# A decoder layer on one core: router logits summed inside the output projection, and expert ranks found on 32 partitions

## The chip, the cores and the metric

The kernel runs on one core of one Trainium2 chip and is written by hand, engine by engine, with semaphores between the engines. The metric is the time of one execution in device microseconds (us). TensorE (PE) multiplies matrices and also transposes 128x128 tiles by a product with an identity; PEld is its weight load. VectorE (DVE), ScalarE (ACT) and GpSimd (POOL) do elementwise work, and SyncE (SP) issues most transfers. Matrix products write to PSUM, eight banks of 128 partitions by 512 float32. Everything else lives in one SBUF array called `arena`; all data are float32.

## The reference

One layer on 512 tokens of width 2048. `h = x + mix(rms_norm(x)) @ w_out`, where `mix` concatenates three token mixers (attention, a state-space layer, a gated recurrence). Then a mixture of experts reads `hn = rms_norm(h, ffn_norm_g)`:

```
gl = hn @ w_group            # 4 groups;  g_idx = argmax
el = hn @ w_router           # 32 experts, 8 in a group
top 2 experts inside the best group; gates = softmax of the two, times p_g
h += sum over the two experts of gate * (silu(hn @ w_gate[e]) * (hn @ w_up[e])) @ w_down[e]
out = rms_norm(h, final_norm_g)
```

The experts' weights are 32 x 3 x 4 MB. All of them are read from HBM once.

## The kernel before, in words

The work is one long sequence of steps (`steps`), walked by every engine in the same order; each engine does its part of a step. PE's products of the input and output projections are laid out in *gaps*: seven products make one pair of column chunks (a Strassen-like scheme, `("pr", p, n)`, line 843 for the output projection), and other steps are hung behind chosen products.

- **Output projection.** Eight pairs `WO_P`, chunks of 128 columns of `h`, each added by DVE to `H0` (rows of tokens, four tiles of 128 tokens by 2048). After a pair, ACT squares its 128 x 128 pieces and accumulates their sums (line 1288). DVE also forms the weight sums of the next products (line 521).
- **Norm and router.** Behind the last pair come DVE's sum of the squares (L1866), ACT's square root (L1367), and for each of four token tiles DVE's `h * rstd * g` into a row buffer `HSB` (L1874). SP writes each row buffer to HBM as `hs_rows` (L611), PE turns it in 16 transposes (L1042, step `hT`), ACT copies these to `HNT` (L1203). Step `rt` (L1048) multiplies the 16 chunks by the router's 36 columns, DVE copies the result (L1883), step `rT` (L1053) turns it back to tokens on partitions, DVE copies it to `RLG` (L1886).
- **Routing on DVE.** Group argmax, two expert argmaxes, one-hots (`onehots_ready`); gates; counts per expert from a product (`rk`, L1059); the *rank* of each expert by count, found on all 128 partitions as a 32 x 32 comparison and a row sum (three instructions, L1931 to L1933); a second 32 x 32 comparison that turns ranks into the order in which experts are loaded (L1422, L1940, L1941, `order_ready`); places of tokens (`id`, L1065) and `slots_ready` (L1997).
- **Experts.** SP waits for `order_ready` and then streams the weights through eight slots of 2 MB (L590); a slot is loaded again when PE has used it. A big and a small expert share a tile of 128 slots: 16 tiles, gate and up (L1124), down (L1143). POOL gathers each tile's rows of `hs_rows` (L763) after `slots_ready`; PE turns them (L1099), DVE copies them from PSUM (L2004), and PE returns results to tokens (`combine`, L1086).

The row buffers, the turned chunks and the router's columns lie where the experts' slots come later.

Of the kernel before, what the change touches and what calls it, by code (L numbers as in the profile page):

```python
# [82 lines left out]
def build(nc, d, out, cc):  # L83

    ctx = ExitStack()
    with ctx:
# [28 lines left out]
        def take(n):  # L115
            at[0] += n
            return at[0] - n
# [7 lines left out]
        LBL, D5, SUB, HNG = take(HH), take(NB5), take(1), take(1)  # L125
# [15 lines left out]
        NPK = KD + 2 * HH + 2  # L141
        assert HNG + 1 - GMIX == NPK
# [70 lines left out]
        JUNK, SSP = AQ + 4 * HB, AQ + 4 * HB + P  # L213
# [4 lines left out]
        HNT = SLOT[6]  # L218
        GF, HSB = E0 + 2048, [E0, E0 + 4096]
        assert SSP + TB * 16 <= GF  # L220
        RLT = GF
        WR = W - KD * 36
# [9 lines left out]
        RKY, RRK, RNB, RSQ, RCP, RBS, RORD = (take(NE) for _ in range(7))  # L232
        RKS, RPX = take(TB * NE), take((TB + 1) * NE)
        assert at[0] <= WR
# [141 lines left out]
        for s in steps:  # L376
# [12 lines left out]
            for x in new:  # L389
# [7 lines left out]
                  "hT", "rt", "rT", "rk", "id")  # L397
# [3 lines left out]
        for at_, s in enumerate(steps):  # L401
            if s[0] == "pq":
                small = [0, 1, 2, 3]
            elif s[0] == "al":
                small, ticking = [0, 1, 2], True
            elif s[0] == "hT":
                small = [0, 1, 2, 3, 4, 5, 6, 7]
# [45 lines left out]
        x_again, h_std, gf_in, hs_ready = sem("x_again"), sem("h_std"), sem("gf_in"), sem("hs_ready")  # L453
        hs_out = [sem("hs_out0"), sem("hs_out1")]
# [108 lines left out]
        def _(sp):  # L563
# [28 lines left out]
            for i in range(len(blocks)):  # L592
# [10 lines left out]
                elif blocks[i][0] == ("wo", 4, 0):  # L603
                    see_copy(sp, ("az", AH - 1))
                    see_copy(sp, ("pr", WO_P[0], 6))
                    sp.dma_start(F(WR, KD * 36), DV(d["router"], 0, [(KD * 36, P), (1, KD * 36)])).then_inc(router_in, 16)
                    sp.dma_start(F(GF, D), DV(d["ffn_norm_g"], 0, [(0, P), (1, D)])).then_inc(gf_in, 16)
                load(i)
            for t in range(TB):
                sp.wait_ge(hs_ready, t + 1)  # L610
                sp.dma_start(DV(hs_d, t * P * D, [(D, P), (1, D)]), F(HSB[t % 2], D)).then_inc(hs_out[t % 2], 16)  # L611

            see_bank(sp, ("rt",))
# [25 lines left out]
        def _(pool):  # L639
# [109 lines left out]
            for s in hs_out:  # L749
                pool.wait_ge(s, 32)  # L750
# [41 lines left out]
        def _(pe):  # L792
# [58 lines left out]
            def do(s):  # L851
# [43 lines left out]
                if kind == "pj":  # L895
# [7 lines left out]
                    return  # L903
                if s not in use:
                    return
# [132 lines left out]
                elif kind == "hT":  # L1038
                    t, q = s[1:]
                    once(hs_ready, t + 1)  # L1040
                    for c in range(4):
                        last = tr(B(bank, [(1, P)], off=c * P), V(HSB[t % 2] + 4 * q + c, [(KD, P)]), ident)  # L1042
                elif kind == "rt":
                    once(router_in, 16)
                    for q in range(16):
                        once_copied(("hT", q // 4, q % 4))
                    for k in range(KD):
                        last = mm(B(bank, [(1, S)], 0, 36), F(WR + k * 36, 36), F(HNT + k * S, S),  # L1048
                                  start=(k == 0), stop=(k == KD - 1))
# [147 lines left out]
        def _(act):  # L1197
# [40 lines left out]
            def do(s):  # L1238
# [29 lines left out]
                elif kind == "fin":  # L1268
# [4 lines left out]
                    for k, j in PAIRS[p]:  # L1273
# [10 lines left out]
                        elif k == "wo":  # L1284
                            for t in range(TB):
                                if j or t:
                                    act.wait_ge(squares_done, j * TB + t)
                                A(F(JUNK, P), F(H0 + t * D + j * P, P), ACT.Square,
                                  accum_out=F(SSP + t * 16 + j, 1)).then_inc(squares_done, 1)
# [66 lines left out]
                elif kind == "hT":  # L1356
                    t, q = s[1:]
                    evac(s, V(HNT + 4 * q * S + t * P, [(S, 4), (1, P)]), ([(P, 4), (1, P)],))

# [4 lines left out]
            for s in steps:  # L1364
                if s == ("hT", 0, 0):
                    act.wait_ge(squares_sum, 1)
                    A(F(STD, TB), F(SSQ, TB), ACT.Sqrt, scale=1.0 / D, bias=F(EPSC, 1)).then_inc(h_std, 1)  # L1367
# [39 lines left out]
        def _(dve):  # L1407
# [367 lines left out]
            def do(s):  # L1775
# [86 lines left out]
                elif kind == "hT" and s[2] == 0:  # L1862
                    t = s[1]
                    if t == 0:
                        dve.wait_ge(squares_done, 16 * TB)
                        v.tensor_reduce(F(SSQ, TB), V(SSP, [(16, TB), (1, 16)]), AX.X, AD).then_inc(squares_sum, 1)  # L1866
                        dve.wait_ge(gf_in, 16)
                        dve.wait_ge(h_std, 1)
                        settle(v.reciprocal(F(RST, TB), F(STD, TB)))
                    if t >= 2:  # L1870
                        dve.wait_ge(hs_out[t % 2], 16)
# [236 lines left out]
```

## Time and profile before

| | us |
|---|---|
| median of 3 runs (2052.52 to 2056.9) | 2055.41 |
| the profiled execution | 2060.28 |
| its span, first to last instruction | 2058.4 |
| end of the last output-projection product | 961.3 |
| first load of expert weights | 1019.6 |
| first expert product | 1049.16 |
| last combine begins | 2028.5 |

Busy shares over the span: PE 93%, DVE 40%, ACT 13%, POOL 9%. HBM moves 251 GB/s on average, but above 410 GB/s from 1020 us to about 2000 us. A time such as 1019.6 is counted from the first instruction of the span.

### The profile page before, as it was taken

The page shows a single profiled execution, that of the slowest core. Times are in us where ns is not written, and L with a number is a line of the kernel's source. Part 1 is how long each engine was busy: PE and PEld are TensorE (multiplying, and loading weights), DVE is VectorE, ACT ScalarE, POOL GpSimd, SP SyncE. Part 2 cuts the span into 40 slices and gives each one's busy share as a digit, 9 for nine tenths or more (in the row PEclk, how much of TensorE's full clock was granted, in tenths as well). Part 3 has the DMA queues.
Part 4 walks back from the last instruction along what each step waited for, and adds up shares of the span by engine and source line. Part 5 has one row for each costly group of instructions (what it writes and reads, how often), then busy time and mean ns, then how long its engine had stood idle before and what let it go on. Part 6 is the DMA issues. An engine that isn't in the chain of part 4 may idle for free.

```text
span 2058.4 us, 32623 instructions
## 1 busy us (share of the span) xinstructions
PE 1906.0 (93%) x13671; PEld 1183.1 (57%) x13671; DVE 821.7 (40%) x1531; ACT 259.6 (13%) x626; POOL 189.1 (9%) x218
## 2 busy tenths in 40 slices
PE   6999999999998979998468999999999999999996
PEld 4888999699987869998122333333333323333332
DVE  6666685176465543333511222212222312222215
ACT  3012112100334231112000000000000000000002
POOL 1353332000000000000010000000000000000000
PEclk9999999999999999999689999999999999999998
DMA  5243333211121233222299999999999999999992
GB/s 208 88 141 99 83 94 96 91 52 60 64 72 47 67 128 109 82 83 78 92 423 425 425 422 423 420 419 422 414 421 406 423 422 411 424 411 423 420 387 105
DMA packets 74419, 508.53 MB, mean 247 GB/s; under 512 B 19200, under 2 KB 19348, under 8 KB 38176
## 3 DMA queue, kind: packets, MB, share of 16 engines
q1 hardware_dynamic: 56720, 486.34, 58.4%
q0 software_dynamic: 5728, 15.81, 2.3%
q10 hardware_dynamic: 11824, 4.17, 1.1%
q8 instruction: 123, 2.02, 0.4%
q14 instruction: 24, 0.20, 0.0%
HBM read 504.26 MB, written 12.99 MB: 251 GB/s over the span
## 4 chain that ended last, share of the span: by engine, by line
PE 77%; DMA 13%; DVE 5%; issue 3%; ACT 2%; SPq 0%; POOL 0%; DVEq 0%; ACTq 0%; POOLq 0%
PE psum L1124 19%; PE psum L843 19%; PE psum L846 15%; DMA arena<-in_moe_w_gate 11%; PE psum L1086 9%; PE psum L1143 6%; PE psum L988 2%; DVE arena L1422 2%; DMA arena<-in_moe_w_down 1%; PE psum L900 1%; PE psum L1099 1%; PE psum L1048 1%; DMA arena<-hs_rows,arena 1%; DVE arena L1425 1%; PE psum L977 0%
## 5 line engine op out<-in xcount | busy, mean ns | idle before, releaser
L1124 PE MATMUL psum<-arena 128*32 128x512 f32 x4096 | 465.9, 608 | 32.6 <-issue 15.9
L843 PE MATMUL psum<-arena 128*128 128x128 f32 x3584 | 411.0, 277 | 2.6 <-issue 2.6
L843 PEld LDWEIGHTS psum<-arena 128*128 128x128 f32 x3584 | 407.8, 194 | 4.1 <-issue 3.6
L1422 DVE TENSOR_TENSOR arena<-psum,arena 128x512 f32<-128x512 f32 x290 | 198.9, 689 | 417.1 <-PE psum L1086 413.9
L1124 PEld LDWEIGHTS psum<-arena 128*32 128x32 f32 x4096 | 135.1, 112 | 355.4 <-issue 354.2
L846 PE MATMUL psum<-arena 128*128 128x256 f32 x1456 | 324.7, 382 | 1.9 <-DVE arena L521 1.4
L846 PEld LDWEIGHTS psum<-arena 128*128 128x128 f32 x1456 | 275.1, 191 | 40.7 <-issue 3.9
L1422 DVE TENSOR_TENSOR arena<-arena,psum 128x256 f32<-128x256 f32 (+2 forms) x174 | 76.5, 439 | 434.9 <-PE psum L843 206.9
L1086 PE MATMUL psum<-arena 128*128 128x512 f32 x512 | 236.0, 605 | 0.9 <-issue 0.9
L1143 PE MATMUL psum<-arena 128*32 128x512 f32 x2048 | 225.9, 599 | 5.7 <-DMA arena<-in_moe_w_down 5.3
L1422 DVE TENSOR_TENSOR arena<-arena 128x128 f32<-128x128 f32 (+17 forms) x448 | 180.1, 443 | 39.8 <-ACT arena L1203 31.3
L1086 PEld LDWEIGHTS psum<-arena 128*128 128x128 f32 x512 | 92.3, 190 | 145.3 <-issue 145.3
L1143 PEld LDWEIGHTS psum<-arena 128*32 128x32 f32 x2048 | 66.6, 111 | 152.9 <-issue 149.7
L521 DVE TENSOR_TENSOR arena<-arena 128x1024 f32<-128x1024 f32 x116 | 148.7, 1282 | 2.5 <-DVE arena L1422 1.3
L775 POOL TENSOR_SCALAR arena<-arena 128x512 f32<-128x512 f32 x16 | 33.3, 2080 | 864.9 <-PE psum L1086 864.6
L2024 DVE COPY arena<-psum 128x512 f32<-128x512 f32 x16 | 11.1, 691 | 190.3 <-PE psum L1143 190.3
L1384 ACT ACTIVATE arena<-psum 128x512 f32<-128x512 f32 x16 | 9.6, 598 | 387.4 <-PE psum L1108 387.4
L1267 ACT ACTIVATE arena<-psum 128x256 f32<-128x256 f32 x50 | 18.9, 378 | 284.9 <-PE psum L846 202.2
L1203 ACT ACTIVATE arena<-psum 128x512 f32<-128x512 f32 (+3 forms) x81 | 38.6, 507 | 110.1 <-PE psum L977 28.8
L1099 PE MATMUL psum<-arena 128*128 128x128 f32 x272 | 37.7, 284 | 14.7 <-DMA arena<-hs_rows,arena 14.7
L1099 PEld LDWEIGHTS psum<-arena 128*128 128x128 f32 x272 | 35.6, 195 | 22.9 <-issue 22.9
L2004 DVE COPY arena<-psum 128x512 f32<-128x512 f32 x68 | 42.4, 681 | 15.1 <-PE psum L1099 15.1
(187 smaller groups left out, 989.1 us busy)
## 6 DMA issues: line engine op xcount, KB each, us to landing
arena<-in_moe_w_gate SPq DMA_DIRECT2D x64, 2048.0 KB, 26.7
arena<-in_moe_w_up SPq DMA_DIRECT2D x64, 2048.0 KB, 26.4
arena<-in_moe_w_down SPq DMA_DIRECT2D x64, 2048.0 KB, 26.3
arena<-in_w_in SPq DMA_DIRECT2D x86, 512.0 KB, 4.6
arena<-in_w_out SPq DMA_DIRECT2D x32, 512.0 KB, 4.7
arena<-in_x SPq DMA_DIRECT2D x8, 1024.0 KB, 8.2
hs_rows<-arena SPq DMA_DIRECT2D x4, 1024.0 KB, 4.0
out<-arena SPq DMA_DIRECT2D x4, 1024.0 KB, 4.0
```

Of the source, the lines that this page charges most:

```text
L521: e.tensor_tensor(F(o, BLK), F(a, BLK), F(b, BLK), ALU.subtract).then_inc(sums_ready, 1)
L775: g.tensor_scalar(F(SEL, S), F(IOTA, S), F(SELP, 1), F(SELP + 1, 1), ALU.is_equal, ALU.mult).then_inc(sel_ready, 1)
L843: last = mm(B(bank, [(1, P)], off=t * P), F(a + t * P, P), F(w + i * P, P), start=start and t == 0, stop=(i == KH - 1), skip_group_check=True)
L846: last = mm(B(bank, [(1, HB)]), F(w + i * P, P), F(a, HB), start=start, stop=(i == KH - 1), skip_group_check=True)
L988: last = mm(B(bank, [(1, P)], off=t * P), F(KT + h * S + t * P, P), F(QT + h * S + t * P, P), start=True, stop=True)
L1086: mm(B(4 + q, [(1, 512)]), F(SEL + t * P, P), F(YSB + q * 512, 512), start=True, stop=True).then_inc(comb_full, 1)
L1099: last = tr(B(TURN_BANK[f], [(1, CAP)], off=c * CAP), V(XG[par] + 4 * f + c, [(KD, P)], 0, CAP), ident)
L1124: last = mm(B(bank, [(1, FE)], 32 * g, 32), F(XT + c * CAP + 32 * g, 32), F(SLOT[slot] + (c % 8) * FE, FE), start=(c == 0), stop=(c == KD ...
L1143: last = mm(B(4 + q, [(1, 512)], 32 * g, 32), F(HTE + m * CAP + 32 * g, 32), F(SLOT[slot] + (m % 2) * D + q * 512, 512), start=(m == 0), s ...
L1203: A(dst, B(bank, dims[0], *dims[1:]), func, **kw).then_inc(free[bank], 1)
L1422: return v.tensor_tensor(o, a, b, op)
L2004: v.tensor_copy(F(XT + 4 * f * CAP, 4 * CAP), B(TURN_BANK[f], [(1, 4 * CAP)])).then_inc(xT_free, 1)
```

## The change

- The router's product no longer waits for the norm. Behind pair *i*+1's second product, PE transposes the two chunks of `h` that pair *i* finished (`ht`, four tiles each), DVE copies them to `HTB`, and behind the fourth product PE adds both chunks' logits (`lg`): chunk 0 to partitions 0 to 63 and chunk 1 to partitions 64 to 127 of PSUM bank 3. The last pair's come after the projection.
- The router's columns are padded from 36 to 64 and multiplied by `ffn_norm_g` once on DVE. `rT` becomes four full products with a 0/1 table, which add the two halves and put tokens on partitions; `1/deviation` is applied to the logits.
- ACT, not DVE, now scales the rows for `hs_rows`, without the gain `g`, into three buffers; the gain is applied when a gathered tile is copied from PSUM (a `tensor_tensor` instead of a copy). POOL's clearing of the gather buffers waits for all four row stores.
- Squares are taken over 256 columns instead of 128, and the table of the square root is asked for early.
- Ranks: small products (`rc`) put counts in rows and columns of 32 partitions; DVE compares, sums and makes a one-hot and a diagonal; product `ro` gives the order of the experts, `rr` spreads the ranks to all partitions. This runs before the gates; six 32 x 32 operations on 128 partitions go.
- SP loads the router's table right behind the second load of `x`, and no longer loads `ffn_norm_g` as rows.

The diff, cut to its core:

```
-        for p in WO_P:
-            gaps += products(p)
+        for i, p in enumerate(WO_P):
+            g = products(p)
+            if i:
+                g[1] += [("ht", i - 1, 0), ("ht", i - 1, 1)]
+                g[3].append(("lg", i - 1))
+            gaps += g
+        gaps.append([("ht", 7, 0), ("ht", 7, 1), ("lg", 7)])
-        steps += [("hT", t, q) for t in range(TB) for q in range(4)]
-        steps += [("rt",), ("rT",), ("rk",), ("id",)]
+        steps += [("rT",), ("rc",), ("ro",), ("rr",), ("rk",), ("id",)]
...
+                if kind == "lg":          # PE
+                    i = s[1]
+                    if i == 0:
+                        take_bank(pe, s)
+                        once(router_ready, 1)
+                    for c in range(2):
+                        once_copied(("ht", i, c))
+                        last = mm(B(3, [(1, S)], 64 * c, 64), F(WR + (2 * i + c) * 64, 64), F(HTB + (2 * (i % 2) + c) * S, S),
+                                  start=(i == 0), stop=(i == 7), skip_group_check=True)
+                    last.then_inc(full[3] if i == 7 else lg_done, 1)
...
+                elif kind == "ht":
+                    i, c = s[1:]
+                    for n in (4, 5, 6):
+                        once_copied(("pr", WO_P[i], n))
+                    for t in range(TB):
+                        last = tr(B(bank, [(1, P)], off=t * P), F(H0 + t * D + (2 * i + c) * P, P), ident)
                 elif kind == "rT":
-                    once_copied(("rt",))
+                    once_copied(("lg", 7))
                     for t in range(TB):
-                        last = tr(B(bank, [(1, 36)], off=t * 36), F(RLT + t * P, P, 0, 36), F(IDENT, 36, 0, 36))
+                        last = mm(B(bank, [(1, 36)], off=t * 36), F(RLT + t * P, P), F(WRS, 36), start=True, stop=True)
+                elif kind == "rc":
+                    for i in range(2):
+                        for t in range(TB):
+                            counts, ones = F(AS + t * NE, NE), F(C["ones"], NE)
+                            last = mm(B(bank, [(1, NE)], 0, NE, off=i * NE), (counts, ones)[i], (ones, counts)[i],
+                                      start=(i == 0 and t == 0), stop=(t == TB - 1), skip_group_check=True)
+                elif kind == "ro":
+                    last = mm(B(bank, [(1, NE)], 0, NE), F(EIDM, NE, 0, NE), F(ROH, NE, 0, NE), start=True, stop=True)
+                elif kind == "rr":
+                    last = mm(B(bank, [(1, NE)]), F(C["ones"], P, 0, NE), F(RDG, NE, 0, NE), start=True, stop=True)
...
+            act.wait_ge(squares_sum, 1)   # ACT, behind the last step
+            A(F(STD, TB), F(SSQ, TB), ACT.Sqrt, scale=1.0 / D, bias=F(EPSC, 1)).then_inc(h_std, 1)
+            act.wait_ge(h_rst, 1)
+            for t in range(TB):
+                if t == 3:
+                    act.wait_ge(hs_out[0], 16)
+                A(F(HSB[t % 3], D), F(H0 + t * D, D), ACT.Copy, scale=F(RST + t, 1)).then_inc(hs_ready, 1)
...
+            s = ("rc",)                   # DVE, right behind onehots_ready
+            settle(v.scalar_tensor_tensor(F(RKY, NE, 0, NE), B(bank, e32, 0, NE, off=NE), float(NE), F(FE_, NE, 0, NE), M, SU))
+            v.scalar_tensor_tensor(F(RNB, NE, 0, NE), B(bank, e32, 0, NE), float(NE), F(RKY, NE, 0, NE), M, ALU.is_lt)
+            settle(v.tensor_reduce(F(RKC, 1, 0, NE), F(RNB, NE, 0, NE), AX.X, AD))
+            ts(F(ROH, NE, 0, NE), F(RKOF, NE, 0, NE), F(RKC, 1, 0, NE), None, ALU.is_equal).then_inc(ranks_ready, 1)
+            ts(F(RDG, NE, 0, NE), F(IDENT, NE, 0, NE), F(RKC, 1, 0, NE), None, M).then_inc(ranks_ready, 1)
+            s = ("ro",)
+            v.tensor_copy(F(ORD, NE, 0, 1).bitcast(I32), B(bank, e32, 0, 1)).then_inc(free[bank], 1)
+            s = ("rr",)
+            v.tensor_copy(F(RRK, NE), B(bank, e32)).then_inc(free[bank], 1)
...
             def turned(n):
                 for f in range(4):
                     dve.wait_ge(xT_full, 4 * n + f + 1)
-                    v.tensor_copy(F(XT + 4 * f * CAP, 4 * CAP), B(TURN_BANK[f], [(1, 4 * CAP)])).then_inc(xT_free, 1)
+                    tt(V(XT + 4 * f * CAP, [(CAP, 4), (1, CAP)]), B(TURN_BANK[f], [(CAP, 4), (1, CAP)]),
+                       V(G2 + 4 * f, [(1, 4), (0, CAP)]), M).then_inc(xT_free, 1)
```

PE's order around the end of the output projection before; L843 are its products, L1042 the transposes of the normed rows, L1048 the router, L1053 and L1059 the turn back and the counts, L1065 the places, L1099 and L1124 the first expert tile:

```order
L843 MATMUL psum<-arena 128x128 x840
L1042 MATMUL psum<-arena 128x128 x64
L1048 MATMUL psum<-arena 36x512 x16
L1053 MATMUL psum<-arena 128x36 x4
L1059 MATMUL psum<-arena 128x128 x2
L1065 MATMUL psum<-arena 128x64 x8
L1099 MATMUL psum<-arena 128x128 x16
L1124 MATMUL psum<-arena 32x512 x128
```

The same end after the change, from the last pair on; L850 are the projection's products, L1061 transposes of `h`, L918 the logits, L1065 the turn back, L1073 to L1080 the rank products, L1086 the counts, L1092 the places:

```order
L1061 MATMUL psum<-arena 128x128 x8
L850 MATMUL psum<-arena 128x128 x32
L918 MATMUL psum<-arena 64x512 x2
L850 MATMUL psum<-arena 128x128 x48
L1061 MATMUL psum<-arena 128x128 x8
L918 MATMUL psum<-arena 64x512 x2
L1065 MATMUL psum<-arena 128x36 x4
L1073 MATMUL psum<-arena 32x32 x8
L1077 MATMUL psum<-arena 32x32
L1080 MATMUL psum<-arena 128x32
L1086 MATMUL psum<-arena 128x128 x2
L1092 MATMUL psum<-arena 128x64 x8
```

Of 64 transposes and 16 router products that stood behind the projection, eight and two are left there; 56 and 14 stand inside it, in seven groups.

DVE's order between two projection products of a middle pair, after the change; L1453 are the sums into `h`, L533 weight sums, L1902 the copies of the transposed chunks (before, the same rows stand without L1902):

```order
L533 TENSOR_TENSOR arena<-arena 128x1024 x2
L1453 TENSOR_TENSOR arena<-arena,psum 128x256
L1902 COPY arena<-psum 128x512 x2
L1453 TENSOR_TENSOR arena<-arena,psum 128x256
L1453 TENSOR_TENSOR arena<-arena 128x2x128
```

The two copies stand behind the sum of the second product and ahead of that of the third.

## Rows read from the trace of the kernel before

**Rows 1.** Windows by stage: busy us of each engine, PEclk, DMA share, GB/s.

```profile
773.50:961.30 187.80, 187.80 (x1680) 187.60 (x1680) 61.87 (x100) 24.92 (x120) 0.00 (x0) 1.00 0.24 81
1164.10:1289.00 124.90, 119.19 (x873) 41.70 (x873) 31.05 (x46) 6.06 (x9) 7.33 (x10) 0.98 1.01 423
1662.40:1785.40 123.00, 118.97 (x872) 41.40 (x873) 31.04 (x46) 6.06 (x9) 7.33 (x10) 0.99 1.00 418
```

**Rows 2.** Timeline of PE: start, us, engine, line, operation, count [idle before <-releaser].

```profile
982.68 16.33 PE L1048 MATMUL psum<-arena 128*36 128x512 f32 x32 [0.78 <-ACT arena L1203]
1026.33 3.65 PE L1065 MATMUL psum<-arena 128*128 128x64 f32 x16 [18.58 <-DVEq L1978]
1044.73 3.65 PE L1099 MATMUL psum<-arena 128*128 128x128 f32 x16 [14.74 <-DMA arena<-hs_rows,arena]
```

**Rows 3.** Timeline of DVE from the projection's end to the tokens' places.

```profile
961.40 0.42 DVE L1422 TENSOR_TENSOR arena<-arena,psum 128x256 f32<-128x256 f32 x1 [2.82 <-PE psum L843]
...
1000.33 0.31 DVE L1886 COPY arena<-psum 128x144 f32<-128x144 f32 x1 [0.59 <-PE psum L1053]
...
1005.71 0.69 DVE L1422 TENSOR_TENSOR arena<-arena 128x128 f32<-128x128 f32 x3
...
1006.84 1.50 DVE L1425 TENSOR_SCALAR arena<-arena 128x4 f32<-128x4 f32 x1
...
1010.20 0.19 DVE L1931 SCALAR_TENSOR_TENSOR arena<-arena 128x32 f32<-128x32 f32 x1
...
1012.94 0.27 DVE L1425 TENSOR_SCALAR arena<-arena 128x32 f32<-128x32 f32 x2
...
1013.70 2.48 DVE L1422 TENSOR_TENSOR arena<-arena 128x1024 f32<-128x1024 f32 x2
...
1017.48 0.18 DVE L1941 CAST arena<-arena 128x32 int32<-128x32 f32 x1
...
1031.08 0.18 DVE L1997 CAST arena<-arena 128x34 uint32<-128x34 f32 x1
```

**Rows 4.** Timeline of SP, the first expert weights.

```profile
1019.60 1.96 SPq L590 DMA_DIRECT2D arena<-in_moe_w_gate  x4
```

**Rows 5.** Chain of waits, expert stage: start, us, engine, line, count.

```profile
1706.69 0.90 PE psum L1099 x8
...
1729.81 3.63 PE psum L1086 x8
1733.44 7.00 PE psum L1124 x64
...
2028.51 13.99 PE psum L1086 x32
```

**Rows 6.** Timeline of PE, expert stage: first tile, four places after a wait, last down.

```profile
1049.16 27.67 PE L1124 MATMUL psum<-arena 128*32 128x512 f32 x256 [0.78 <-DVE arena L2004]
...
1091.53 9.67 PE L1143 MATMUL psum<-arena 128*32 128x512 f32 x64 [5.26 <-DMA arena<-in_moe_w_down]
...
1225.80 7.07 PE L1124 MATMUL psum<-arena 128*32 128x512 f32 x64 [1.11 <-DMA arena<-in_moe_w_gate]
...
1475.98 7.07 PE L1124 MATMUL psum<-arena 128*32 128x512 f32 x64 [2.00 <-DMA arena<-in_moe_w_gate]
...
1785.42 8.77 PE L1124 MATMUL psum<-arena 128*32 128x512 f32 x64 [3.98 <-issue]
...
2013.68 13.94 PE L1143 MATMUL psum<-arena 128*32 128x512 f32 x128
```

**Rows 7.** Timeline of DVE: scaled turns of `x`, and copies of a gathered tile.

```profile
24.07 4.27 DVE L1422 TENSOR_TENSOR arena<-psum,arena 128x512 f32<-128x512 f32 x7
...
2012.17 2.47 DVE L2004 COPY arena<-psum 128x512 f32<-128x512 f32 x4
```

**Rows 8.** Groups by line (busy, mean ns) and an issue row (KB, us to landing).

```profile
L1211 ACT ACTIVATE arena<-arena 128x2048 f32<-128x2048 f32 x8 | 15.2, 1902 | 7.7 <-DVE arena L1422 7.7
...
hs_rows<-arena SPq DMA_DIRECT2D x4, 1024.0 KB, 4.0
```

More of the change, by code:

```diff
@@ L231, in build @@
             take(n) for n in (NE, NE, NE, NAS, NAS, NAS, NAS, NE * NE, NOV + 1))
-        RKY, RRK, RNB, RSQ, RCP, RBS, RORD = (take(NE) for _ in range(7))
+        RKY, RRK, RNB, RSQ, RCP, RBS, ROH, RDG = (take(NE) for _ in range(8))
+        RKC = take(1)
         RKS, RPX = take(TB * NE), take((TB + 1) * NE)
-        assert at[0] <= WR
+        assert at[0] <= W
         XG, YSB, XT = [E0, E0 + 2048], E0 + 4096, E0 + 6144
@@ L405, in build @@
                 small, ticking = [0, 1, 2], True
-            elif s[0] == "hT":
-                small = [0, 1, 2, 3, 4, 5, 6, 7]
+            elif s[0] == "pr" and s[1] == WO_P[0]:
+                small, ticking = [0, 1, 2], False
+            if s[0] == "lg":
+                use[s] = (3, uses[3])
+                uses[3] += s[1] == 7
+                continue
             if s[0] == "pr":
@@ L452, in build @@
         l_ready, e_ready, w_ready, ao_ready = sem("l_ready"), sem("e_ready"), sem("w_ready"), sem("ao_ready")
[L453 to L454 removed]
+        x_again, h_std, h_rst, hs_ready = sem("x_again"), sem("h_std"), sem("h_rst"), sem("hs_ready")
+        router_ready, lg_done, ranks_ready = sem("router_ready"), sem("lg_done"), sem("ranks_ready")
+        hs_out = [sem(f"hs_out{i}") for i in range(3)]
         squares_done, squares_sum = sem("squares_done"), sem("squares_sum")
@@ L748, in _ @@
             pool.wait_ge(onehots_ready, 1)
-            for s in hs_out:
-                pool.wait_ge(s, 32)
+            for i, s in enumerate(hs_out):
+                pool.wait_ge(s, 32 if i == 0 else 16)
             for x in XG:
@@ L1283, in do @@
                             A(x, x, ACT.Sigmoid).then_inc(gated, 1)
-                        elif k == "wo":
+                        elif k == "wo" and j % 2 == 0:
+                            i = j // 2
                             for t in range(TB):
[L1286 to L1289, printed above, removed]
+                                if i or t:
+                                    act.wait_ge(squares_done, i * TB + t)
+                                else:
+                                    A(F(SM, 1), F(EPSC, 1), ACT.Sqrt)
+                                A(F(JUNK, 2 * P), F(H0 + t * D + j * P, 2 * P), ACT.Square,
+                                  accum_out=F(SSP + t * 8 + i, 1)).then_inc(squares_done, 1)
                 elif kind == "w1T":
@@ L1861, in do @@
                     attn_out(AH - 1)
[L1862 to L1871, printed above, removed]
-                        for q in range(4):
-                            see_bank(dve, ("hT", t - 2, q))
-                    v.scalar_tensor_tensor(F(HSB[t % 2], D), F(H0 + t * D, D), F(RST + t, 1), F(GF, D), M,
-                                           M).then_inc(hs_ready, 1)
+                elif kind == "ht":
+                    i, c = s[1:]
+                    if i == 0 and c == 0:
+                        dve.wait_ge(router_in, 16)
+                        tt(V(WR, [(64, KD), (1, 64)]), V(WR, [(64, KD), (1, 64)]), V(WRG, [(1, KD), (0, 64)]),
+                           M).then_inc(router_ready, 1)
+                    if i >= 2:
+                        dve.wait_ge(lg_done, i - 1)
+                    bank = see_bank(dve, s)
+                    v.tensor_copy(F(HTB + (2 * (i % 2) + c) * S, S), B(bank, [(1, S)])).then_inc(free[bank], 1)
+                elif s == ("lg", 7):
+                    dve.wait_ge(squares_done, 8 * TB)
+                    v.tensor_reduce(F(SSQ, TB), V(SSP, [(8, TB), (1, 8)]), AX.X, AD).then_inc(squares_sum, 1)
+                    bank = see_bank(dve, s)
+                    v.tensor_copy(F(RLT, S), B(bank, [(1, S)])).then_inc(free[bank], 1)
+                    dve.wait_ge(h_std, 1)
+                    v.reciprocal(F(RST, TB), F(STD, TB)).then_inc(h_rst, 1)
@@ L1962, in _ @@
                 settle(v.tensor_reduce(F(RPF + k * TB, TB), V(RTMP, all3), AX.X, AD))
-            for t in (2, 3):
-                for q in range(4):
-                    see_bank(dve, ("hT", t, q))
-                dve.wait_ge(hs_out[t % 2], 32)
+            dve.wait_ge(hs_out[2], 16)
             ge = V(RGE_T, [(NT + 1, NAS), (1, NT + 1)])
```

101 lines of the change are left out of this document (49 added, 52 removed).

## The prediction

> **What bounds the kernel now.** I read the page first, then the windows by stage, then the timelines of PE, DVE and SP from the end of the output projection to the first expert tile, and last the chain of waits through the experts.
>
> Three stages matter. In the output projection PE is busy for 187.80 of 187.80 us at full clock while DVE is busy 61.87 and ACT 24.92 [rows 1]: whatever PE gets here lengthens the stage one for one, and what DVE and ACT get is hidden. The last DVE sum into `h` ends at 961.82; the logits lie with tokens on partitions at 1000.64, the one-hots at 1006.40, the load order at 1017.66, the places at 1031.26 [rows 3]. Hardly any expert work runs in that time, so it is all path. From there two paths run into the experts: SP's first load at 1019.60 [rows 4], 1.9 us behind the load order, and PE's first expert product at 1049.16 [rows 6], 17.9 us behind the places, most of it the gather that PE waited 14.74 us for [rows 2].
>
> In the expert stage PE and the weight transfers are nearly level. Two tiles take PE 123.0 us, the loop's own stall of 3.98 us included, at 418 GB/s [rows 1, 6]; early on they take 124.9 at 423 GB/s [rows 1], and PE waited for weights 5.26, 1.11 and 2.00 us [rows 6]. Two tiles need 24 loads of 2.1 MB and some 1 MB of gathered rows, 51.4 MB, 121.5 us at 423 GB/s. So up to tile 7 (1475.98) the transfers, which start at 1019.60 and never pause, decide; from there PE does. Both starts have to be moved to gain, and the smaller move counts, with up to 5.26 + 1.11 + 2.00 us of waits and 9.67 - 7.00 = 2.7 us of a slow restart to be won back where the transfers get ahead [rows 5, 6]: 11 us.
>
> **Added inside the projection.** Seven groups of eight transposes and two logit products. Eight transposes at full clock take 0.90 us (L1099 [rows 5]). A plain 128x512 product takes 13.99 / 16 = 0.87 us [rows 5]; the experts' four 32-column products side by side take 7.00 / 32 = 0.22 each [rows 5]. Two 64-column products side by side should lie at 0.44 each: I take 0.87 for the pair, with 0.44 and 1.75 as ends. Going from one width of product to the other and back costs 3.63 - 13.99 / 4 = 0.14 us [rows 5]. Sum: 7 x (0.90 + 0.87 + 0.14) = +13.4 us, between 7 x 1.34 = 9.4 and 7 x 2.9 = 20.
>
> That change of width is where a rule of the Trainium skill speaks against the change. "TensorEngine Tiling (Array Packing)", Key Properties, says that switching between tiling modes drains TensorE. The trace agrees that it costs something, the 0.14 us above. By that row it is 1 us in all; only if a drain cost two orders more would it cancel the change.
>
> DVE's 16 copies of 128x512 cost 2.47 / 4 = 0.62 us each [rows 7], about 1.4 us in a pair of 25 us of which it works a third: hidden. PE meets them two products (7 us) after the transposes, so it does not wait. The one scaling of the router's table (128x1024, half of the 2.48 us of two such in [rows 3]) and ACT's wider squares are hidden by PE too. The router's load, 0.6 MB behind `x`, has 25 us and more: DMA share is 0.24 [rows 1]. If DVE were late, each us would be a us of PE.
>
> **The end of the projection.** Before, 961.82 to 1000.64: 38.8 us. It goes: the squares' tail, four scalings with their store waits, 64 transposes, and 16.33 us of router products that began on a slow clock [rows 2, 3]. What is left: a handoff 0.15; first four transposes and copy about 1.0; second copy 0.85; handoff 0.15; the last chunk's product 0.87; copy to SBUF 0.7; four full products against the 36-column table, eight records of 128-column weights, 0.9 (at 0.11 each) to 1.8 (at the cold 3.65 / 16 = 0.23 [rows 2]); scaling 0.3 and handoffs 0.3. That is 5.5 to 6.7 and I take 6.2: -32.6 us. The four squares and the root run beside it. On a slow clock throughout it would be 8.5.
>
> **Load order.** From one-hots to load order was 11.3 us. Now: eight small products (16 records: 1.2 us, or 3.65 at the cold row; I take 2.4, since their weights are a quarter to a half as wide), four small DVE steps 0.9, one product and a copy 0.6, handoffs 0.4: 4.3 us, so -7.0 (between -5.7 and -8.2). SP then needs its 1.9 us as before. SP stands behind the four row stores: ACT scales at 1.9 us a tile, and the fourth waits for the first store's landing, 4.0 us [rows 8]. That gives 1.9 + 4.1 + 0.3 + 1.9 = 8.3 us after the deviation, some 2 us before the load order is there. Nothing more is late, but a store 3 us slower would show.
>
> **Places.** Six DVE instructions of 32x32 elements go: 1010.20 to 1012.94 and 1013.70 to 1017.57, 6.6 us. The rank chain, `rr` included, is put in front of the gates and costs 4.65. So places come 1.95 us sooner after the one-hots. The gates need ACT's exponential, which now stands behind the four scalings and a table load; it is ready about 1 us before DVE wants it. One DVE step took 1.50 us where its neighbours take 0.2 [rows 3], beside POOL's clearing of the gather buffers. The clearing now waits for the last row store and meets other DVE steps: the same 1.3 us, 0 to 3.6 for its 3.6 us.
>
> That stall fits the Trainium skill, "SBUF — State Buffer", on the port pair that DVE and GpSimd share under an exclusive lock; it only moves here.
>
> **Sum.** Weights start at +13.4 - 32.6 - 7.0 = -26.2 us. PE starts at +13.4 - 32.6 - 1.95 = -21.1 us. The transfers get 5.1 us ahead, PE's first wait of 5.26 goes, and then the transfers hold it until tile 7: the end follows the weights' start, -26.2, and a little of the slow restart, -0.3. In the profiled execution 2060.3 - 26.5 = 2033.8; that one lies 4.9 us above the median, so on the median 2055.4 - 26.5 = 2029 us.
>
> The gain `g` in `turned` turns four copies a tile into `tensor_tensor` with a repeated operand. The same form at the start took 4.27 / 7 = 0.61 us, the copy takes 0.62 [rows 7]: nothing. PE needs the third and fourth in the down products that reuse their banks: these begin at 2013.68, an eighth of the 13.94 us (1.74 [rows 6]) later come the third's, at 2015.4, and the copies end at 2014.64 with the fourth, at about 2014.0 with the third. So 1.4 us of slack.
>
> **Rivals.**
> 1. *PE, not the transfers, holds the expert stage.* The weights start 5 us further ahead and all 11 us of waits and slow restart vanish: -21.1 - 11.1 = -32.2, 2023 us; with the projection's low end 2019. For it: the transfers are faster by 1.5 us in two tiles when both run freely [rows 1]. Against it: waits came back at 1225.80 and 1475.98 after the first was over [rows 6].
> 2. *Groups inside the projection cost more.* The 64-column products do not run side by side, and each group makes PE slow down: +20 instead of +13.4; with the cold ends of the two small chains (+2.3 and +1.3): -26.5 + 10.5 = -16, 2039 us. For it: no 64-column product of full depth into two halves is in the trace. Against: the 32-column ones pack fully.
> 3. *Slower: the scaled copy sits between two tiles.* PE's down products wait for the turn's banks. The third may end 1.4 us later, so each copy may be 0.4 us longer before PE waits; beyond that four times the excess, 16 times over. It cancels the gain at 26.5 / 16 = 1.7 us a tile, that is with copies of 0.62 + 0.4 + 0.4 = 1.4 us, and at 1.8 us each the time is about 2055 - 26 + 51 = 2080. Against it stands the 0.61 of the same form [rows 7]; the repeated operand there is read the same way.
> 4. *The load order gains nothing*: SP, held by row stores or by the exponential's neighbours, starts no earlier after the one-hots. Then the weights start at -19.2, and the end follows: 2036 us.
>
> **How the numbers follow.** My forecast, 0.52, holds 2025 to 2033. Rival 1 has 0.17, rival 2 0.14, rival 4 0.11, rival 3 0.03, a change that does nothing measurable 0.03. The range 2017 to 2040 takes in the low end of rival 1 and all of 2 and 4, and leaves out 0.1 to 0.15. A measurement tells 0.2%, 4 us, from no change: faster 0.94, same 0.02, slower 0.04 (rival 3 and something unseen).
>
> **What would show it.** Projection: PE still without gaps, about 201 us where 187.8 stood, the logit pair 0.87 us apart from start to end (1.75 means rival 2). From last sum to `RLG` about 6 us. First weight load about 993.5 (1019.6 - 26.2), first expert product about 1028. No 5 us wait in the first down product, waits of 1 to 4 us up to tile 7 (none: rival 1). Copies of a gathered tile at 0.62 to 0.69 us. I am wrong if the projection grows by more than 20 us, if weights start later than 1001, or if two late tiles no longer take 123 us.

## The result, and the profile after

The changed kernel takes 2042.45 us (median of 5, 2040.63 to 2045.12) where the kernel before takes 2055.41 (5, 2052.52 to 2059.35): a ratio of 0.9936, 95% interval 0.9922 to 0.995. It is faster by 0.6%, which is 13 us and not the 26.5 forecast, and lies 2.5 us outside the range.

Up to the experts the sum came as forecast: the projection and SP's first load a little worse, the steps between a little better. The timeline of PE after the change, from the end of the projection (L1061 transposes of `h`, L918 logits, L1073 rank products, L1092 places, L1126 and L1151 the first expert tile):

```profile
974.18 1.06 PE L1061 MATMUL psum<-arena 128*128 128x128 f32 x8 [0.67 <-DVE arena L1453]
975.66 1.67 PE L918 MATMUL psum<-arena 128*64 128x512 f32 x4 [0.42 <-DVE arena L1902]
...
985.53 1.03 PE L1073 MATMUL psum<-arena 128*32 128x32 f32 x16 [6.27 <-issue]
...
1000.38 3.65 PE L1092 MATMUL psum<-arena 128*128 128x64 f32 x16 [10.78 <-DVEq L2021]
1018.83 3.65 PE L1126 MATMUL psum<-arena 128*128 128x128 f32 x16 [14.80 <-DMA arena<-hs_rows,arena]
1023.27 27.67 PE L1151 MATMUL psum<-arena 128*32 128x512 f32 x256 [0.78 <-DVE arena L1453]
```

The first expert product starts 25.9 us sooner (1049.16 in [rows 6]); the 16.33 us of L1048 in [rows 2] are gone. DVE in the same stretch (last sum into `h`, scaled logits, one-hots, load order, places):

```profile
973.62 0.42 DVE L1453 TENSOR_TENSOR arena<-arena,psum 128x256 f32<-128x256 f32 x1 [2.82 <-PE psum L850]
...
979.30 0.31 DVE L1453 TENSOR_TENSOR arena<-psum,arena 128x144 f32<-128x144 f32 x1 [1.15 <-PE psum L1065]
...
984.68 0.69 DVE L1453 TENSOR_TENSOR arena<-arena 128x128 f32<-128x128 f32 x3
...
987.93 0.18 DVE L1960 CAST arena<-psum 1x32 int32<-1x32 f32 x1 [0.32 <-PE psum L1077]
...
1005.13 0.18 DVE L2040 CAST arena<-arena 128x34 uint32<-128x34 f32 x1
```

They answer to [rows 3]: 5.6 us from the last sum to `RLG` instead of 38.8, 2.7 from one-hots to load order instead of 11.3, 19.9 from one-hots to places instead of 24.9. SP, row stores and first weights:

```profile
980.21 6.80 SPq L619 DMA_DIRECT2D hs_rows<-arena  x4
991.35 1.97 SPq L602 DMA_DIRECT2D arena<-in_moe_w_gate  x4
```

The first weights are 28.25 us sooner than in [rows 4]. And yet the last combine of the timeline, which began at 2028.51 [rows 5], begins only 19.8 us sooner:

```profile
1062.45 8.77 PE L1170 MATMUL psum<-arena 128*32 128x512 f32 x64 [2.08 <-DMA arena<-in_moe_w_down]
...
1135.97 7.07 PE L1151 MATMUL psum<-arena 128*32 128x512 f32 x64 [1.43 <-DMA arena<-in_moe_w_gate]
...
1386.89 4.26 PE L1151 MATMUL psum<-arena 128*32 128x512 f32 x22 [3.67 <-issue]
1392.56 5.31 PE L1151 MATMUL psum<-arena 128*32 128x512 f32 x42 [1.41 <-issue]
...
1512.05 5.34 PE L1151 MATMUL psum<-arena 128*32 128x512 f32 x22 [3.90 <-issue]
1517.71 5.31 PE L1151 MATMUL psum<-arena 128*32 128x512 f32 x42 [0.32 <-issue]
...
2008.73 13.97 PE L1113 MATMUL psum<-arena 128*128 128x512 f32 x32 [0.89 <-issue]
```

Here is what is new. PE's loop makes seven passes of two tiles. The first, at 1135.97, is entered without a jump back, and the other six begin behind one. Before, each of these six began with one stop of about 4 us, and then 64 records in one piece (1785.42 in [rows 6]). In the last four nothing was waited for; in the first two the profile puts the stop down to a weight transfer:

```profile
1289.00 9.93 PE L1124 MATMUL psum<-arena 128*32 128x512 f32 x64 [4.49 <-DMA arena<-in_moe_w_gate]
...
1413.43 8.77 PE L1124 MATMUL psum<-arena 128*32 128x512 f32 x64 [4.08 <-DMA arena<-in_moe_w_gate]
```

Now the 64 records behind each jump back are cut: 22, a second stop of 0.3 to 1.4 us, then 42. The first pass has neither stop. A pass behind a jump back takes 124.3 to 125.5 us, where the late ones took 123.0 to 123.6 (the last is shorter in either kernel, 122.1 now and 119.9 before). PE's waits added up, from 1024 to 2010 us, after the change:

```profile
PE psum L1151 <- issue: 29.8, 12, 4.2
PE psum L1151 <- DMA arena<-in_moe_w_gate: 7.3, 3, 3.1
PE psum L1170 <- DMA arena<-in_moe_w_down: 2.1, 1, 2.1
```

and of the kernel before, in the same stretch (columns: us in total, times, longest):

```profile
PE psum L1124 <- issue: 15.9, 4, 4.1
PE psum L1124 <- DMA arena<-in_moe_w_gate: 15.8, 5, 4.5
...
PE psum L1143 <- DMA arena<-in_moe_w_down: 5.3, 1, 5.3
```

By these rows the waits for transfers fell by 11.7 us and the stops without a cause rose by 13.9. But the 4.49 and 4.08 us above stand at jumps back, where the changed kernel has its stops too, so they are better counted as stops. Then the waits for transfers fell from 12.5 to 9.4 us, the six stops at the jumps back took 24.5 and now 23.5, and the six second stops are new, 6.3 us together. From the first expert product to the last combine PE takes 6.1 us longer (979.35 before, 985.46 after). So the gain was given back inside PE's loop, whose text the change does not touch.

### The profile page after: what moved, and what is told of

The parts are those of the page before. It is cut to its first block, busy times and chain, and to the rows that moved or that the text cites. A ratio compares the mean times of both kernels' runs of the same rounds, so it can differ in the third digit from the quotient of the medians.

```text
span 2038.7 us, 32619 instructions
## 1 busy us (share of the span) xinstructions
PE 1899.3 (93%) x13695; PEld 1176.1 (58%) x13695; DVE 817.7 (40%) x1544; ACT 249.8 (12%) x551; POOL 189.5 (9%) x218
## 4 chain that ended last, share of the span: by engine, by line
PE 80%; DMA 10%; DVE 4%; issue 3%; ACT 2%; SPq 0%; DVEq 0%; POOL 0%; POOLq 0%; ACTq 0%
PE psum L1151 21%; PE psum L850 19%; PE psum L853 15%; PE psum L1113 10%; DMA arena<-in_moe_w_gate 9%; PE psum L1170 7%; DVE arena L1453 2%; PE psum L1006 2%; PE psum L907 1%; PE psum L1126 1%; DMA arena<-hs_rows,arena 1%; DVE arena L1456 1%; PE psum L995 0%; DVE arena L2092 0%; PE psum L967 0%
## 5 line engine op out<-in xcount | busy, mean ns | idle before, releaser
L1151 PE MATMUL psum<-arena 128*32 128x512 f32 x4096 | 471.0, 607 | 37.9 <-issue 29.8
L1453 DVE TENSOR_TENSOR arena<-psum,arena 128x512 f32<-128x512 f32 x359 | 240.5, 687 | 443.4 <-PE psum L1113 423.9
L850 PE MATMUL psum<-arena 128*128 128x128 f32 x3584 | 412.9, 277 | 2.6 <-issue 2.6
L850 PEld LDWEIGHTS psum<-arena 128*128 128x128 f32 x3584 | 407.8, 194 | 9.8 <-issue 9.3
L1151 PEld LDWEIGHTS psum<-arena 128*32 128x32 f32 x4096 | 133.3, 112 | 367.3 <-issue 366.1
L1453 DVE TENSOR_TENSOR arena<-arena,psum 128x256 f32<-128x256 f32 (+2 forms) x174 | 76.5, 440 | 439.1 <-PE psum L850 211.3
L1453 DVE TENSOR_TENSOR arena<-arena 128x128 f32<-128x128 f32 (+17 forms) x446 | 177.8, 440 | 38.3 <-ACT arena L1230 30.1
L533 DVE TENSOR_TENSOR arena<-arena 128x1024 f32<-128x1024 f32 x116 | 148.8, 1282 | 2.5 <-DVE arena L1453 1.3
L2068 DVE COPY arena<-psum 128x512 f32<-128x512 f32 x16 | 11.1, 692 | 186.3 <-PE psum L1170 186.3
L1415 ACT ACTIVATE arena<-psum 128x512 f32<-128x512 f32 x16 | 9.6, 598 | 387.4 <-PE psum L1135 387.4
L1126 PE MATMUL psum<-arena 128*128 128x128 f32 x272 | 37.7, 284 | 14.8 <-DMA arena<-hs_rows,arena 14.8
L1126 PEld LDWEIGHTS psum<-arena 128*128 128x128 f32 x272 | 35.6, 195 | 23.0 <-issue 23.0
L1418 ACT ACTIVATE arena<-psum 128x512 f32<-128x512 f32 x32 | 19.1, 597 | 208.9 <-PE psum L1170 208.9
L1230 ACT ACTIVATE arena<-psum 128x512 f32<-128x512 f32 (+3 forms) x65 | 29.8, 484 | 101.3 <-PE psum L995 28.8
```

The source lines that it names most:

```text
L533: e.tensor_tensor(F(o, BLK), F(a, BLK), F(b, BLK), ALU.subtract).then_inc(sums_ready, 1)
L850: last = mm(B(bank, [(1, P)], off=t * P), F(a + t * P, P), F(w + i * P, P), start=start and t == 0, stop=(i == KH - 1), skip_group_check=True)
L1126: last = tr(B(TURN_BANK[f], [(1, CAP)], off=c * CAP), V(XG[par] + 4 * f + c, [(KD, P)], 0, CAP), ident)
L1151: last = mm(B(bank, [(1, FE)], 32 * g, 32), F(XT + c * CAP + 32 * g, 32), F(SLOT[slot] + (c % 8) * FE, FE), start=(c == 0), stop=(c == KD ...
L1230: A(dst, B(bank, dims[0], *dims[1:]), func, **kw).then_inc(free[bank], 1)
L1453: return v.tensor_tensor(o, a, b, op)
```

## The experiments

My theory (A): PE's stops hang on where the loop lies in PE's instruction stream. After the jump back PE stops for 4 us; the instructions behind some boundary in the stream arrive at a fixed time later, and if PE reaches the boundary sooner, it stops again. The change put 24 product records, 24 weight loads and some waits ahead of the loop (the page of the profile counts 13,671 of each on PE before, 13,695 after), and so moved the boundary into the first group. Rivals: the scaled copies cost it (B), or the earlier weights collide with something in the tiles (C). The kernel before took 2055.2 us in the first four comparisons (9 runs) and 2055.44 in the last three (23 runs).

**1. The changed kernel with its loop moved.**

```
+            for _ in range(28):
+                tr(B(2, [(1, P)]), ident, ident)
             turn(0, 0, 0, (0, 1, 2, 3), True)
```

Here `tr` is one transposing product on PE with its weight load: 56 instructions in PE's wait for the gather.

> The changed kernel with 28 transposes of the identity put on PE between the places and the first turn, in PE's 14.8 us wait for the gathered rows. Theory A (the expert loop of the changed kernel pays for where its PE instructions lie: after the loop's own stall PE stops a second time, 22 product records into the first part, for 0.3 to 1.4 us plus a slow restart, 125.0 us for two tiles in place of 123.1): 56 more instruction records ahead of the loop move that spot, the second stop goes, two tiles take 123.1 us again, first expert product unchanged near 1023, the run about 8 to 10 us below the changed kernel, 2033. Theory B (the scaled copy, or transfers, set the 125.0): nothing changes, 2042, second stop at record 22 as before.

Measured: 2030.54 us (4 runs, 2029.05 to 2032.9), ratio 0.9879 (0.9863 to 0.9894). PE gets more to do and the kernel is 11.9 us faster than the changed one. The timeline has one stop a pass again, the 64 records in one piece:

```profile
1512.92 8.45 PE L1151 MATMUL psum<-arena 128*32 128x512 f32 x64 [4.08 <-issue]
1635.70 8.49 PE L1151 MATMUL psum<-arena 128*32 128x512 f32 x64 [4.06 <-issue]
```

122.8 us a pass. The group's 64 records end 8.5 us after its start in these passes; in the changed kernel the 22 and 42 with the stop between them took 11.0 (1512.05 to 1523.02). That is 2.5 us a pass, part of it hidden by waits for weights in the early passes. Theory A holds. B and C both fall: the copies are as they were, and so is the start of PE against the weights (first expert product 31.7 us behind the first load, 31.9 in the changed kernel).

**2. The kernel before with its loop moved the other way**, so that the boundary should fall into its first group: the same two lines with `range(26)`.

> The kernel before with 26 such transposes on PE ahead of the first turn, hidden in its wait for the gather. Theory A: the changed kernel had 48 more product and weight-load records and some waits ahead of its loop, so this brings the loop of the kernel before to about the same place: a second stop inside the first part of each pass of the loop appears, two tiles take 125 us from tile 8 on, and the run is 6 to 12 us slower than before, about 2064. Theory B: no change, 2055.

Measured: 2063.49 us (5 runs, 2060.2 to 2066.72), ratio 1.0039 (1.0024 to 1.0055). The second stop appears in a kernel that has nothing of the change:

```profile
1414.86 4.15 PE L1124 MATMUL psum<-arena 128*32 128x512 f32 x23 [3.99 <-issue]
1420.79 4.88 PE L1124 MATMUL psum<-arena 128*32 128x512 f32 x41 [1.78 <-issue]
...
1539.64 4.47 PE L1124 MATMUL psum<-arena 128*32 128x512 f32 x23 [3.68 <-issue]
1545.30 4.88 PE L1124 MATMUL psum<-arena 128*32 128x512 f32 x41 [1.19 <-issue]
```

The 52 instructions are 26 records with their weight loads, so without them the boundary would lie behind record 49 (23 + 26). At 64 records in 8.77 us PE is there, by estimate, some 6.7 us after the pass's first product, later than the 5.9 and 5.7 at which the stops end here. That fits the kernel before, which shows none.

**3. The changed kernel with plain copies in `turned`** (the gain `g` is left out of the experts' input).

```
-                    tt(V(XT + 4 * f * CAP, ...), B(TURN_BANK[f], ...), V(G2 + 4 * f, ...), M).then_inc(xT_free, 1)
+                    v.tensor_copy(F(XT + 4 * f * CAP, 4 * CAP), B(TURN_BANK[f], [(1, 4 * CAP)])).then_inc(xT_free, 1)
```

> The changed kernel, with the gathered tile copied from PSUM by a plain copy (the gain g is left out of the experts' input). Theory A: no change, 125 us for two tiles, second stop still there, 2042. Theory B, the scaled copy holds PE: 123.1 us for two tiles, 2033.

Measured: 2043.21 us (4 runs, 2038.76 to 2046.95), ratio 0.9949 (0.9932 to 0.9965), the same as the changed kernel. The scaled copy costs nothing that can be measured here, and the second stops stay:

```profile
1384.33 4.39 PE L1151 MATMUL psum<-arena 128*32 128x512 f32 x22 [3.59 <-issue]
1389.84 5.31 PE L1151 MATMUL psum<-arena 128*32 128x512 f32 x42 [1.13 <-issue]
```

**4. The changed kernel with PE's loop written out**, the other engines' loops kept. This takes away the jumps back, and with them whatever PE computes for a pass.

```
-            with pe.Fori(1, NPAIR // 2) as it:
+            for it in range(1, NPAIR // 2):
```

> The changed kernel with PE's loop over the expert tiles written out, the other engines' loops left. Theory A: PE has no branch there, so both the 4 us stop at each pass, the slow restart (8.8 in place of 7.0 us for the first part) and the second stop go; PE needs about 117.4 us for two tiles, and the transfers (51.4 MB at 424 GB/s, 121.3 us) bind: expert stage about 16 to 28 us shorter, 2014 to 2026. If the stops have another cause than the branch (a wait for slots, the clock), they stay and the time is 2042.

Measured: 2021.64 us (5 runs, 2020.56 to 2023.92), ratio 0.9839 (0.9826 to 0.9853). No stop without a cause is left between the tiles; PE waits for weights alone, twelve times:

```profile
PE psum L1151 <- DMA arena<-in_moe_w_gate: 28.7, 12, 4.5
PE psum L1113 <- issue: 0.9, 1, 0.9
```

This version beats both kernels: 33.6 us below the kernel before.

**5. The changed kernel with its loop moved half as far**: `range(14)` in experiment 1.

> After with 14 transposes of the identity on PE before the loop over tiles (half of the 28 that took the second stop away). The work is the same, only the place of the loop's first instruction moves by 28 instructions. Theory A (PE stops where it runs into a part of the instruction stream that has not been fetched yet, and that part arrives at a fixed time after the loop's jump): the stop moves from behind record 22 to behind record 8 of the first product group (22 - 14), and lasts until the same moment, some 5.7 us after the group's start, so about 4 us instead of 1.4 at the most. The pass of two tiles becomes about 127 us instead of 125, seven passes make +14 to +16, the time 2056 to 2059 us. Theory A2 (the fetch starts only when PE gets there and always takes the same): the stop moves to record 8 and stays 1 to 1.4 us, the time stays 2042. Theory B (the second stop comes from data or another engine, and the 28 transposes removed it by a shift in time): the stop stays behind record 22, or is gone, 2030 to 2042.

Measured: 2059.68 us (12 runs, 2056.77 to 2061.39), ratio 1.002 (1.0006 to 1.0033). Fourteen idle transposes, in a stretch where PE waits for a gather anyway, cost 17 us and make the changed kernel slower than the one before. The stop moved from behind record 22 to behind record 8:

```profile
1389.87 1.06 PE L1151 MATMUL psum<-arena 128*32 128x512 f32 x8 [4.13 <-issue]
1395.30 9.10 PE L1151 MATMUL psum<-arena 128*32 128x512 f32 x56 [4.36 <-issue]
...
1518.71 1.94 PE L1151 MATMUL psum<-arena 128*32 128x512 f32 x8 [4.04 <-issue]
1524.36 7.72 PE L1151 MATMUL psum<-arena 128*32 128x512 f32 x56 [3.71 <-issue]
```

It ends 5.4 and 5.7 us after the pass's first product; in the changed kernel 5.7 and 5.7 (1386.89 to 1392.56, 1512.05 to 1517.71), in experiment 2 5.9 and 5.7. That is the fixed arrival of theory A: the end of the stop stands still to within some tenths, and its start moves with the place. The five full passes behind a jump back take 128.2 us on average, 1.2 more than I expected; I had left out the clock after a 4 us stop. The 56 records behind it took 7.5 to 9.1 us at a mean granted clock of 0.68 to 0.83. The changed kernel's 42 records, behind stops of 0.3 to 1.4 us, took 5.31 us at 1.00 in each pass.

**6. The kernel before with PE's loop written out**: the edit of experiment 4.

> Before with PE's loop over tiles written out (the other engines' loops kept), the counterpart of the written-out after (2021.64). Theory A: no stall of 4 us at the jump, the weight transfers never meet a late slot and decide alone. With the same 997.3 us from the first weight load to the last combine as in the written-out after, and a first load 28.2 us later, 2049 to 2051 us: the change by itself is worth 28 us and not the 13 measured, and the difference was lost to the loop on PE. Rival (the change is worth only about 13 us whatever the loop does, because PE's or DVE's own work in the expert stage became longer): 2035 us.

Measured: 2046.22 us (12 runs, 2041.47 to 2049.45), ratio 0.9958 (0.9944 to 0.9971). With both loops written out the change is worth 24.6 us, with both left as they are 13.0: the rival's 2035 us falls. In the profiles the stage from the first weights to the last combine is 999.58 us here and 999.47 in experiment 4 (989.20 to 1988.67):

```profile
1011.14 1.96 SPq L590 DMA_DIRECT2D arena<-in_moe_w_gate  x4
```

```profile
2010.72 13.97 PE L1086 MATMUL psum<-arena 128*128 128x512 f32 x32 [0.89 <-issue]
```

Without the stops the end follows the weights' start to 0.1 us. My 2049 to 2051 was 3 us too high. Its 997.3 us were reckoned from the changed kernel's first load (991.35) and not from experiment 4's own (989.20), and its 28.2 us held 2.3 that came from upstream. With 28.2 - 2.3 = 25.9 the sum is 2047.5; what is left is told below, under the sum.

**7. The written-out changed kernel with the old ranks.** Steps `rc`, `ro`, `rr` go, and L1931 to L1933 and L1938 to L1941 of the kernel before come back. The edit, cut to its core:

```
-        steps += [("rT",), ("rc",), ("ro",), ("rr",), ("rk",), ("id",)]
+        steps += [("rT",), ("rk",), ("id",)]
```

> The written-out after with the ranks found as in before: no rank products, the 32 x 32 comparisons on 128 partitions behind the gates and counts, the load order last. The router inside the projection stays. Theory A (the first weight load sets the end): from one-hots to load order 11.3 us instead of 2.7, less the 1.3 us that SP then no longer stands behind the row stores: +7.3, 2029 us. Rival (PE's start decides): the places come only about 1 us later, and the time is 2022 to 2024.

Measured: 2030.85 us (6 runs, 2029.68 to 2033.96), ratio 0.9888 (0.9868 to 0.9908). The rank products are worth 9.2 us of the 24.6, the router inside the projection the rest. It is 1.9 us above my sum, and DVE shows why. From one-hots to load order takes 13.0 us here and not 11.3: the gates' sum comes right behind the one-hots in this order, and waits 2.85 us for ACT's exponential, which stands behind the row scalings:

```profile
990.69 0.17 DVE L1933 TENSOR_REDUCE arena<-arena 128x4 f32<-128x16 f32 x1 [2.85 <-ACT arena L1390]
```

So the two halves of the change help each other: the rank chain fills the time in which that exponential is late.

## Why the prediction was wrong

**The steps before the experts were right.** The projection: forecast +13.4 us. PE is still without gaps, for 202.4 us where 187.8 stood [rows 1]:

```profile
771.10:973.50 202.40, 202.37 (x1764) 195.69 (x1764) 71.96 (x115) 17.44 (x65) 0.00 (x0) 1.00 0.21 69
```

That is +14.6, or 2.09 us for each group instead of 1.91. DVE's sums of one pair after the change show where:

```profile
791.13 0.42 DVE L1453 TENSOR_TENSOR arena<-arena,psum 128x256 f32<-128x256 f32 x1 [4.33 <-PE psum L850]
795.57 0.42 DVE L1453 TENSOR_TENSOR arena<-arena,psum 128x256 f32<-128x256 f32 x1 [1.69 <-PE psum L850]
799.15 0.42 DVE L1453 TENSOR_TENSOR arena<-arena,psum 128x256 f32<-128x256 f32 x1 [2.69 <-PE psum L850]
803.86 0.42 DVE L1453 TENSOR_TENSOR arena<-arena,psum 128x256 f32<-128x256 f32 x1 [4.29 <-PE psum L850]
```

and the same sums before:

```profile
793.46 0.42 DVE L1422 TENSOR_TENSOR arena<-arena,psum 128x256 f32<-128x256 f32 x1 [4.33 <-PE psum L843]
797.03 0.42 DVE L1422 TENSOR_TENSOR arena<-arena,psum 128x256 f32<-128x256 f32 x1 [3.15 <-PE psum L843]
800.61 0.42 DVE L1422 TENSOR_TENSOR arena<-arena,psum 128x256 f32<-128x256 f32 x1 [2.69 <-PE psum L843]
804.11 0.42 DVE L1422 TENSOR_TENSOR arena<-arena,psum 128x256 f32<-128x256 f32 x1 [3.08 <-PE psum L843]
```

The first distance grew by 0.87 (4.44 for 3.57, the transposes, forecast 0.90) and the third by 1.21 (4.71 for 3.50, the logits, forecast 0.87 + 0.14). So the pair of 64-column products does run side by side, and rival 2's 1.75 is out, but pair and change of width together cost 1.21 and not 1.01: +1.2 us in all. If the pair itself takes the 0.87 of a full product, 0.34 is left for the change of width instead of 0.14; no run takes the two apart. The logits and the order came sooner than forecast (5.6 for 6.2; 2.7 for 4.3, the narrow products ran in 1.03 us and not 2.4); SP took 3.2 us behind the load order and not 1.9. In experiment 7, where the order comes some 10 us later, SP needs 1.9 again (1000.80 to 1002.72), so the other 1.3 us are probably SP still busy with the row stores. The places gained 4.9 and not 1.95: the rank chain cost 3.3 instead of 4.65, and the 1.50 us step of [rows 3] is 0.14 now. The prediction had its stall move to other steps; no DVE step beside POOL's clearing (992.02 to 995.60) is visibly longer, and why it vanished is not shown. To compare with the forecast, what came from upstream has to be taken off; both profiles have the same product (first of before, then of after)

```profile
750.48 5.68 PE L843 MATMUL psum<-arena 128*128 128x128 f32 x28
```

```profile
748.15 5.68 PE L850 MATMUL psum<-arena 128*128 128x128 f32 x28
```

2.3 us apart before any changed instruction that matters. That is chance: in the nine profiles this product starts between 745.99 and 750.62, in both kernels. So the weights' start gained 28.25 - 2.33 = 25.9 us, against 26.2 forecast. Such closeness is in part luck, since the errors of the terms cancel: +1.2 in the projection, -0.6 up to the logits, -1.6 up to the order, +1.3 at SP. PE's start gained 25.9 - 2.3 = 23.6 us against 21.1 forecast.

**The step that failed** is in the prediction's paragraph on the expert stage and in its sum: up to tile 7 the transfers decide, "from there PE does", with two tiles of PE fixed at 123.0 us, and then "the end follows the weights' start". I took those 123.0 us, "the loop's own stall of 3.98 us included", for a property of the tile's work. They were a property of where the loop lay: with the same work they became 125 in the changed kernel, 128.2 in experiment 5 and 122.8 in experiment 1. The prediction said it would be wrong "if two late tiles no longer take 123 us", and they took 125. It gave no rival in which instructions ahead of the loop change the loop. The size: experiment 1 gives 11.9 us for the second stops and the slower passes around them. Rival 3 asked for a loss between the tiles too, but by the copies, and experiment 3 excludes these: at 0.69 us and a pitch of 0.85 they fit as before.

```profile
1019.96 0.69 DVE L1453 TENSOR_TENSOR arena<-psum,arena 128x512 f32<-128x512 f32 x1 [14.65 <-PE psum L1126]
1020.82 0.69 DVE L1453 TENSOR_TENSOR arena<-psum,arena 128x512 f32<-128x512 f32 x1 [0.16 <-PE psum L1126]
```

Smaller slips of the prediction change nothing in this. The difference 3.63 - 13.99 / 4 is 0.13 and not 0.14, and a group with the pair at 1.75 comes to 2.8 and not 2.9. The waits it counted, 5.26, 1.11 and 2.00, leave out the 4.09 us ahead of the loop's first pass (1164.14 in the kernel before), which fell to 1.43.

**Sum.** Forecast -26.5, second stops +11.9, rest +1.6: -13.0. With one loop's place made harmless the kernel takes 2030.5, 1.5 us above the forecast. That rest has a likely source. The 26.5 were worked out against a profiled execution 4.9 us above its median. From the product at 750 us to the first weights that execution took 269.1 us, and so did experiment 2 (269.1), but experiment 6, with the same code up to there, took 264.6. The difference lies at the end of what the change removes: in the longer form the fourth row waited for its store and PE's router products ran 16.33 us, in the shorter they ran

```profile
976.65 13.89 PE L1048 MATMUL psum<-arena 128*36 128x512 f32 x32 [0.89 <-ACT arena L1203]
```

The granted clock in these products was 1.00, and 0.85 in the longer form. So the kernel before has two forms there, 4.5 us apart, and the change ends both at 243.2 us in each of its profiles with the new ranks (five). How often each form comes in executions without a profile is open; if the median is of the shorter kind part of the time, the change is worth correspondingly less than 25.9 there, as in experiment 6 (24.6).

**What the stops are.** The runs show that moving 28 PE instructions moves the second stop by 14 records of products (each with its weight load), that its end is bound to the jump back, and that it goes where the loop is written out. They show too that the first stop hangs on the jump: the same instructions in the first pass, entered without one, have neither stop. Whether that stop is the jump itself or what PE does with its registers beside it is open, since writing the loop out removes both.

A mechanism that fits stands in the Trainium skill. "Runtime: NRT & Kernel Launch", section "Instruction fetch mechanics", says that each engine's instructions are fetched ahead strictly in order, in blocks of 256, that a taken branch to a target outside of what is held forces a fetch before execution goes on, and that crossing a block is otherwise mostly hidden. These runs agree on the branch (3.6 to 4.2 us each time) and differ on the crossing, if the second stop is one: it is hidden in straight code, but within the first 5 to 6 us after a jump back it cost 0.2 to 4.4 us. That the boundary is a block of just that size is consistent with 28, 52 and 56 instructions doing what they did, but no run here measured the size, nor saw the fetches themselves.

## What to carry to other kernels

A loop on the engine that sets the time can pay at each jump back, as this one did, and pay a second time if the first microseconds of a pass run into instructions that have not arrived; an edit ahead of such a loop can then move the time by many times its own length (here 2042, 2060 and 2031 us with 0, 28 and 56 more instructions in a wait). Look for stops without a releaser at the same record of each pass, and compare two versions with the loop written out, or at more than one place. Before savings are summed against one profiled execution, see whether the stretch that goes takes as long in a second one.

## What the runs showed of the hardware that was not expected

- The end of the second stop after a jump back is nearly fixed: 5.1 to 5.9 us after the pass's first product, with 8, 22 or 23 records run before it. The one exception, 4.6 us in experiment 3, is a pass whose first product had itself waited 4.49 us for weights. Counted from the end of the last product ahead of the jump the stop ends after 8.9 to 10.0 us in every pass, that one included.
- Written out, the expert stage takes 999.4 to 999.6 us from the first weight load to the last combine in three different kernels (experiments 4, 6, 7); with the loop it took 1007.5, 1008.9, 1017.4 and 1036.8 (experiment 1, before, after, experiment 5).
- Two 64-column products of depth 128 and 512 columns of data, into the two halves of a bank, run side by side; with both changes of width the pair costs 1.21 us among full products, where one full product takes 0.87.
